# A recurrence that turns its values to rows by a matrix which takes away their head's mean

## The reference, cut to what matters

```
def step(state, inp):
    r_t, w_t, k_t, v_t, aa_t, bb_t = inp
    sa = jnp.einsum('bhvk,bhk->bhv', state, aa_t)
    state = state * w_t[:, :, None, :] + sa[..., None] * bb_t[:, :, None, :] + v_t[..., None] * k_t[:, :, None, :]
    return state, jnp.einsum('bhvk,bhk->bhv', state, r_t)
...
mean = jnp.mean(y, axis=-1, keepdims=True)
var = jnp.mean(jnp.square(y - mean), axis=-1, keepdims=True)
y = ((y - mean) * lax.rsqrt(var + GN_EPS)).reshape(b, s, c) * lnx_w + lnx_b
bonus = (jnp.sum(r_h * k_h * r_k, axis=-1, keepdims=True) * v_h).reshape(b, s, c)
return ((y + bonus) * g).astype(z.dtype)
```

## Time and profile before

| | us |
|---|---|
| median of 3 runs | 2418.88 (2418.67 to 2420.12) |
| the profiled execution, its own time | 2418.01 |
| its span, first to last instruction | 2416.7 |
| PE busy in the span | 2328.0 (96%) |
| granted clock of PE, mean | 0.986 |

### The profile page before, as it was taken

The page is one execution under the profiler, slowest core; times in us unless marked ns, Lnnn a source line. Parts: engine busy times, 40 slices in busy tenths (PEclk is TensorE's granted clock), DMA queues, the critical chain, the costliest instruction groups (busy, mean ns, idle before and its releaser), DMA issues.

```text
span 2416.7 us, 33857 instructions
## 1 busy us (share of the span) xinstructions
PE 2328.0 (96%) x14384; PEld 1836.3 (76%) x14384; DVE 1434.3 (59%) x1782; ACT 691.2 (29%) x864; POOL 884.0 (37%) x418
## 2 busy tenths in 40 slices
PE   6999999799999999799999999999999999999998
PEld 4776776577776787588888777888878888888887
DVE  5222323678877513767675588788843467888633
ACT  3122122443443423222222233322222333222212
POOL 4313221111111344444444444444444434444442
PEclk8999999899999999899999999999999999999999
DMA  6433332212122243233333223333332323333331
GB/s 238 133 105 102 113 94 77 57 47 52 46 48 48 64 143 93 60 101 100 97 112 89 79 83 104 96 96 96 103 105 84 102 79 87 96 97 99 114 91 54
DMA packets 412038, 222.56 MB, mean 92 GB/s; under 512 B 33823, under 2 KB 409458, under 8 KB 410610
## 3 DMA queue, kind: packets, MB, share of 16 engines
q1 hardware_dynamic: 383074, 206.14, 29.5%
q10 hardware_dynamic: 28816, 14.27, 2.2%
HBM read 214.61 MB, written 5.77 MB: 91 GB/s over the span
## 4 chain that ended last, share of the span: by engine, by line
PE 89%; DVE 6%; DMA 2%; ACT 1%; issue 1%; POOL 1%; SPq 1%; ACTq 0%; DVEq 0%; POOLq 0%
PE bank L312 88%; PE bank L315 1%; SPq L1514 0%; DMA rw_sixteen<-inverses 0%; DMA inverses<-rw_solved 0%; DVE h_low L2096 0%; DMA w_raw<-in_w_att_out 0%; DVE g_c L2302 0%; POOL w_low L308 0%; DVE sq L664 0%; DVE rw_keep L1480 0%; DVE sq L660 0%; DVE rw_terms L1566 0%; DMA vec_rows<-in_c 0%; DVE sq L566 0%
## 5 line engine op out<-in xcount | busy, mean ns | idle before, releaser
L308 POOL TENSOR_TENSOR w_low<-w_raw,w_high 128x1024 fp32r<-128x1024 f32 (+1 forms) x331 | 849.4, 2568 | 1462.2 <-ACT w_high L301 1462.2
L312 PE MATMUL bank<-h_high,w_high 128*128 128x512 f32 x2008 | 809.2, 403 | 25.8 <-DVE h_low L671 9.6
L312 PE MATMUL bank<-h_low,w_high 128*128 128x512 f32 x2008 | 787.5, 392 | 0.0
L301 ACT CAST w_high<-w_raw 128x1024 fp32r<-128x1024 f32 (+1 forms) x331 | 358.6, 1085 | 885.7 <-PE bank L312 863.5
L312 PE MATMUL bank<-h_high,w_low 128*128 128x512 f32 x2008 | 510.2, 393 | 0.0
L312 PEld LDWEIGHTS bank<-h_high,w_high 128*128 128x128 f32 x2008 | 379.1, 189 | 132.2 <-issue 27.1
L312 PEld LDWEIGHTS bank<-h_high,w_low 128*128 128x128 f32 x2008 | 376.0, 188 | 84.4 <-issue 5.3
L312 PEld LDWEIGHTS bank<-h_low,w_high 128*128 128x128 f32 x2008 | 379.9, 189 | 78.7 <-issue 4.1
L312 PE MATMUL bank<-g_high,w_high 128*128 128x512 f32 x352 | 139.1, 395 | 2.3 <-ACT g_c L2281 2.3
L312 PE MATMUL bank<-g_low,w_high 128*128 128x512 f32 x352 | 138.9, 395 | 0.0
L2174 DVE TENSOR_TENSOR x_res<-bank,x_res 128x512 f32<-128x512 f32 x32 | 22.1, 689 | 168.4 <-PE bank L312 168.3
(11 more groups left out here) (375 smaller groups left out, 2820.4 us busy)
## 6 DMA issues: line engine op xcount, KB each, us to landing
w_raw<-in_w_in SPq DMA_DIRECT2D x54, 512.0 KB, 4.9
w_raw<-in_w_up SPq DMA_DIRECT2D x44, 512.0 KB, 3.8
w_raw<-in_w_ffn_gate SPq DMA_DIRECT2D x44, 512.0 KB, 3.8
w_raw<-in_w_ffn_up SPq DMA_DIRECT2D x44, 512.0 KB, 3.9
w_raw<-in_w_ffn_down SPq DMA_DIRECT2D x32, 704.0 KB, 4.5
w_raw<-in_w_ada SPq DMA_DIRECT2D x32, 512.0 KB, 3.8
w_raw<-in_w_in ACTq DMA_DIRECT2D x25, 512.0 KB, 4.1
w_raw<-in_w_down SPq DMA_DIRECT2D x16, 704.0 KB, 4.5
```

The lines of the kernel that those rows point to most:

```text
L301: self.A.copy(self.w_high[:, u % SPLIT_SLOTS, 0:k * P], self.raw_of(key)[:, 0:k * P]).then_inc(*self.S.rounded(*key))
L308: self.G.tensor_tensor(self.w_low[:, slot, 0:k * P], self.raw_of(key)[:, 0:k * P], self.w_high[:, slot, 0:k * P].bitcast(F32), ALU.subtrac ...
L312: return self.T.matmul(out, lhsT, rhs, start=start, stop=stop, skip_group_check=True)
```

## The change

Three edits:

- A constant matrix `R.centre` of 128x128 is filled at setup: 63/64 on the diagonal, -1/64 elsewhere in a head's 64x64 block, 0 outside. POOL does it with one memset and three selects.
- In `arrive_pe` the four transposes of v become four f32 products of 128x128, with the v tile as weights and `R.centre` as the moving matrix, into the same bank 7. `v_tok` then holds v less its head's mean, by tokens. The channel-by-token v tile, which the bonus uses, stays as it is.
- `mean_pe` goes, with the subtraction L1795 and its wait; `square_y_dve` keeps the square alone.

```
+        R.centre = sb("rw_centre", [P, P])
...
+        self.same_block(R.centre[:], HEAD, -1.0 / HEAD)
+        self.band(R.centre[:], ALU.not_equal, 0, [[-1, P]], 1, 1.0 - 1.0 / HEAD)
...
             for j in range(4):
-                ins = self.turn(self.bank[b][:, j * P:(j + 1) * P], sources[what](j))
+                out = self.bank[b][:, j * P:(j + 1) * P]
+                if what == "v":
+                    ins = self.mm(out, sources[what](j), R.centre[:], j == 0, j == 3)
+                else:
+                    ins = self.turn(out, sources[what](j))
...
-    def mean_pe(self, i):
-        self.T.wait_ge(*self.S.dve_close.at("y", i))
-        self.mm(self.bank[4][:], self.head_ones[:], self.rw.y, True, True).then_inc(*self.S.close_pe("mean", i))
-
-    def mean_y_dve(self, i):
+    def square_y_dve(self, i):
         V, S_, R = self.V, self.S, self.rw
-        V.wait_ge(*S_.close_pe.at("mean", i))
-        V.wait_ge(*self.own("dve"))
-        V.scalar_tensor_tensor(R.y, self.bank[4][:], -1.0 / HEAD, R.y, ALU.mult, ALU.add).then_inc(*S_.dve_close())
         V.wait_ge(*self.own("dve"))
         V.tensor_tensor(R.y2, R.y, R.y, ALU.mult).then_inc(*S_.dve_close("square", i))
...
-            next(receptance, None)
-            if has(i):
-                self.mean_pe(i)
-            next(receptance, None)
-            next(receptance, None)
+            run(islice(receptance, 3))
```

2 lines of the change are left out of this document (1 added, 1 removed).

## The result

The changed kernel took 2427.72 us (median of 10 executions, 2423.50 to 2433.91), the kernel before, measured beside it, 2421.10 (10 executions, 2418.67 to 2426.51). The ratio is 1.0029, 95% interval 1.0018 to 1.0041: slower by 0.3%, outside the range of 2416.5 to 2423.8. The same changed kernel was measured twice more, with 1.0013 (1.0003 to 1.0022) and 1.0026 (1.0015 to 1.0037). Over all three it is 2427.2 us in 28 executions, against 2421.1 in the 134 of the kernel before that stood beside some kernel of this study (2416.3 to 2429.7), so 6.1 us more. The three measurements by themselves give 6.6, 3.4 and 7.8 us. The three executions that the forecast stood on had shown 2418.67 to 2420.12, much less spread than there is.

A forecast was written before the change was run, and what follows sets the result against it. It took PE's stream and two trains of work on other engines to end together in each turn. 7 x 0.35 us for v, less 0.86 in turn 7, gave +1.6 on 2418.88: 2420.5 us, range 2416.5 to 2423.8.

The forecast's parts named there:

- setup: Filling the matrix at setup: one memset and three selects on POOL, ahead of its 14.59 us idle time; cost 0.
- The mean's product gains nothing in turns 0 to 5: Product of 0.86 us on PE ahead of the next key's square; removal gains 0 to 0.04 us a turn, taken as 0.
- In turn 7 it gains 0.86: Last turn, without the mean's product: variance and ACT's work move up, PE's 0.96 us wait keeps its length; gain 0.86 us.
- The subtraction costs nothing: Removing DVE's L1795 (0.69 us) and its wait, counted at nothing; at most 8 x 0.69 = 5.5 us if cover were gone.
- The v group grows by 0.39 and 0.04 of it is absorbed: v products on PE ahead of the bonus product: loss 0.35 us in each of turns 0 to 6, bounds 0.30 and 0.43.
- The v group of pair 0 costs nothing: The eighth v group, before turn 0: DVE waits 0.72 us for the blocks' landing, more than 0.43, so cost 0.
- The rival about instructions: PE's instruction stops in the turns, 3.2 us together, vanish (2417.3) or come in every turn (2423.7); chance 0.12.
- The sign that it named as wrong: Turns differing among each other by over 0.5 us from before would point to instruction stops or transfers, not counted work.
- The base: Starting time of the forecast: profiled execution 2418.01, median of the runs shown 0.87 above it, so 2418.88 us.
- the shown spread of 1.45 us: Spread of the runs shown; half of it was put below 2417.3 to set the range's lower end at 2416.5.
- The price of the f32 product: Rival: f32 product costs four times a transpose, v group 1.72 us, +7.9 us in all, 2426.8; chance 0.06.

## Why the prediction was wrong

The sum said +1.6 us. Counted again with what the runs showed, and beside it what the prediction had (the 1.0 and 1.5 are estimates, from the three and the two traces of the table and from the kernels with pair 0's group twice and with four transposes more, where the first solve is 0.9 to 1.0 us late and turn 0 is 1.2 to 2.0 us longer):

```
                                        predicted   shown
turns 0 to 6, longer v group            7 x 0.35    7 x 0.40 = 2.8
v group of pair 0: the late load        0           1.0
  and the low clock in turn 0           0           1.5
mean's product, turns 0 to 6            0           0
mean's product, turn 7                  -0.86       -0.87
setup                                   0           0
subtraction, turn 3                     0           0.35
sum                                     +1.6        +4.8
measured, pooled                                    +6.1
```

Point by point:

- **The mean's product gains nothing in turns 0 to 5, since PE meets L1291 to within 0.04 us.** Right, to the hundredth: six waits of 0.81 us have come in its place, with the product put back they go and the turns stay the same, and turns 2 and 4 of the kernel that only drops the mean are those of before. At the end of turn 6 the wait for the landing swallows it: the last solve waits 1.02 us, where it waited 0.15. What it did not foresee is turn 0, where without the product a fetch falls on the store of the inverses, which lands 0.3 to 1.7 us later.
- **In turn 7 it gains 0.86.** Right, 0.87, with PE's wait of 0.96 us unchanged.
- **The subtraction costs nothing.** For its time this holds. But in turn 3 DVE is 0.35 us late without it, which nothing in the prediction foresaw; the cause is open.
- **The v group grows by 0.39 and 0.04 of it is absorbed.** The mechanism was right and the size a little off. It grew by 0.45 us. The row that I took it from, four products in 0.82 us, ended at a product of another kind, and the two prices bracketed 0.39 to 0.43, not 0.45. 0.05 us were absorbed. Seven turns give 0.35 us more in all.
- **The v group of pair 0 costs nothing, since DVE waits 0.72 us for the blocks.** This is the step that failed. The wait did cover the group's time, it went from 0.72 to 0.25 us. What it didn't cover was its number of instructions. They move PE's fetch of 16 KB from behind the first solve into SP's eight loads, where one load then takes 0.9 us longer to issue; the landing is as late, PE waits 1.5 to 2.0 us and not 1.2, and up to 3.4 us behind it run at 1.2 GHz. The prediction put this term at 0, and it measured about 2.5 us. Four idle transposes alone bring all of it, and sixteen take it off the loads again.
- **The rival about instructions** named the right resource and the wrong victim. It counted PE's own stops in the turns. A fetch also goes with a slow issue or landing of SP's transfers, and those stood on the path. The sign that it named as wrong, turns that differ from before by more than 0.5 us among each other, did come.
- **The base.** The forecast was put on a median of three executions, 2418.88. Of 134 executions the median is 2421.1. That is 2.2 of the 7.2 us by which 2427.7 misses 2420.5, and has nothing to do with the change. The page even showed a granted clock of 0.986, near the upper end: over the 299 executions of this study with a clock on record, with each kernel's own level, a mean clock lower by 0.001 goes with 1.66 us more (95% interval 1.52 to 1.80), and it ranges from 0.980 to 0.988. Half of "the shown spread of 1.45 us" was no bound for that.
- **The price of the f32 product**, the slower side of the forecast, was no cause: 0.89 against 0.44 us is a factor of two, not four, and the kernel with plain transposes made twice is as slow. The rule of the Trainium skill on transposes ("Perfetto Trace Analysis", section "Transposes") pointed the right way with this: the group did get longer on the path.

What stays open is 6.1 - 4.8 = 1.3 us, no more than the three measurements differ by among each other. Two effects of the fetches lie in turns 0 and 1 and nearly cancel in the traces. The store of the inverses in turn 0 takes 2.97, 2.72 and 4.19 us to land, where it took 2.49 and 2.47, and the one in turn 1 takes 2.81, 2.80 and 2.64, where it took 3.29 and 3.22: 0.8 us lost and 0.5 won. The rest stands in turns 5 and 6, which are 2.8 us longer on the mean where 0.8 is counted, but they differ among the three executions by 4 us. Two of the three have a longer stop for instructions in turn 5 than the kernel before, whose stop is the last of these rows:

```profile
724.59 0.33 PE L312 MATMUL bank<-rw_keep,rw_work 64*64 64x64 f32 x2 [1.85 <-issue]
```

```profile
724.20 0.47 PE L312 MATMUL bank<-rw_keep,rw_work 64*64 64x64 f32 x2 [1.78 <-issue]
```

```profile
717.41 0.27 PE L315 MATMUL bank<-ident,x_res 128*128 128x128 f32 x1 [0.72 <-issue]
```

The same two have a stretch at 1.2 GHz behind the solve of turn 6. Windows of the changed kernel and of before behind a wait of 1.9 and of 1.8 us:

```profile
751.00:759.00 8.00, 6.91 (x78) 5.29 (x79) 4.48 (x9) 3.17 (x4) 0.00 (x0) 0.79 0.01 2
```

```profile
741.00:749.00 8.00, 6.22 (x93) 4.96 (x94) 6.12 (x11) 3.26 (x5) 0.00 (x0) 1.00 0.12 18
```

One of the two has another such stretch inside turn 5. With up to 1.7 us for each (half of 3.4, an estimate) they make most of the surplus. The remaining execution has a stop of 0.81 us and no such stretch, although PE waits 1.96 us there, and its two turns are nearly as counted. Whether the stretches come from the moved fetches wasn't tried. The kernel with the setup alone, whose PE stream is that of the kernel before, has one in turn 6 too, behind a stop of 1.60 us, and a turn 6 of 46.89 us in place of 44.92. So they also come without the change, and that the change makes them more frequent is argued, not shown.

## What to carry to other kernels

In this kernel an edit of PE's stream had two prices, its time and its number of instructions, and the second was paid where the fetches came to lie: before an edit is costed at nothing because its time is hidden, look where the instruction packets fall against short chains of transfers that are issued one by one. Time taken out of a stream just ahead of a wait that another engine sets is not gained, and a weight load that is held while its product shows no idle time was the sign of it here. And a difference of 0.2% needs the spread of the kernel before from tens of executions, not three.

## What the runs showed of the hardware

- **A fetch of instructions goes with a slow issue on another queue.** In 11 traces a 16 KB packet of queue 8 fell among SP's eight loads of the first inverses, and each time one load took 1.08 to 1.94 us to issue in place of 0.45. In the 9 traces without it all eight took at most 0.45. In the second trace of the changed kernel the packet took 0.96 us, from 464.28; the load ahead of it landed at 466.57, 1.03 us behind the one before, where they follow at 0.5 us otherwise, and the issue at 464.25 took 0.94 us longer than the others. The Trainium skill, "DMA: Bandwidth & Descriptors", section "Queues, rings and completion order", has a DMA engine change between queues only where a packet ends. That the long packet therefore holds up the short ones of a load, and with them the issue of the next, is my reading of it, and no run tried it. The same is seen at the stores of the blocks: in the kernel before the ones issued at 482.72 and 529.02 took 2.13 and 1.70 us in place of 0.43, with fetches at 482.92 and 529.04.
- **It also goes with a slow landing.** Of the 140 stores of the inverses in turns 0 to 6 of the 20 traces, 24 had a fetch that started within 1.4 us behind their issue. They landed 2.38 to 4.19 us behind it, 19 of them later than 2.6 us. The other 116 landed in 2.37 to 2.58 us.
- **PE's stops for instructions follow fetches.** From the first solve to the end of the recurrence the 20 traces have 60 stops of PE for instructions of over 0.25 us, and each begins 0.4 to 2.5 us after such a fetch has started; the longest was 2.12 us. They fall where PE runs through many small products.
- **The number of instructions places the fetches.** In both executions of the kernel before the fetch came at the same place of PE's stream, 1.05 and 0.96 us and 64 PE records behind the start of the first solve, though one was 3.3 us later than the other. With 8 records more ahead of it, in kernels as different as those with four products in the group, with four transposes more in it and with four idle ones, it came 10 to 12 records ahead of that start.
- **The clock.** The stretches at 1.2 GHz around the first solve lasted 3.4, 6.8 or 10.2 us. One of 3.4 us costs up to 1.7 us where PE is busy, by the ratio of the two levels (an estimate). Behind the first solve it came with 10 of the 11 late loads, after waits of PE of 1.4 to 2.5 us (in the eleventh the stretch ended 0.9 us ahead of the solve), and in the nine others, after waits of 0.5 to 1.4 us, the clock was full but for their first microsecond at most. But behind the solve of turn 6, waits of 1.9 to 2.5 us were followed by either.
- **An f32 product of 128x128 against a transpose**: 0.11 us a record for both, two records for the product and one for the transpose.
